# One row of mLSTM forget sums, spread over 128 partitions by TensorE instead of by a DMA from DRAM

## The reference, cut to what matters

```
b = jnp.cumsum(fb, axis=-1)
D = jnp.where(causal, b[..., :, None] - b[..., None, :] + ib[..., None, :], -jnp.inf)
inter = b + m[..., None]
m_t = jnp.maximum(inter, D.max(-1))
s_mat = jnp.exp(D - m_t[..., None]) * jnp.einsum('bhtd,bhsd->bhts', qb, kb)
num = (w_inter[..., None] * jnp.einsum('bhtd,bhde->bhte', qb, C) + jnp.einsum('bhts,bhse->bhte', s_mat, vb))
```

## Time and profile before

| quantity | value |
|---|---|
| median of 3 runs | 1026.46 us (1025.17 to 1029.41) |
| the profiled execution, its own time | 1025.17 us |
| its span, first to last instruction | 1023.4 us |
| TensorE, matmuls | 953.4 us busy, 93% |
| VectorE | 602.2 us busy, 59% |
| ScalarE | 457.2 us busy, 46% of the span |
| mean granted TensorE clock | 0.981 |

### The profile page before, as it was taken

How to read it: one execution, slowest core, us unless ns; L and a number is a source line. 1 busy time by engine, 2 the same in 40 slices (tenths; PEclk the granted TensorE clock), 3 DMA queues, 4 the chain that set the end, 5 groups by cost and what they waited for, 6 DMA issues and landing times.

```text
span 1023.4 us, 14224 instructions
## 1 busy us (share of the span) xinstructions
PE 953.4 (93%) x4965; PEld 754.4 (74%) x4965; DVE 602.2 (59%) x1100; ACT 457.2 (45%) x811; POOL 173.0 (17%) x145
## 2 busy tenths in 40 slices
PE   2399999899999899998999998999999999988995
PEld 1367877677877688776788776788778888866883
DVE  2854786564875566865657856553653333264766
ACT  1133456554475463665554765434743222251221
POOL 1101021322032231122420132311100000001220
PEclk9689999999999999999999999999999999999998
DMA  8702121011311102211113111115712111233232
GB/s 287 250 11 67 43 63 42 22 34 29 93 40 41 31 20 61 72 40 31 30 31 93 42 31 33 31 50 165 242 58 73 50 42 41 93 105 101 83 105 100
DMA packets 78083, 73.64 MB, mean 72 GB/s; under 512 B 4792, under 2 KB 66360, under 8 KB 78044
## 3 DMA queue, kind: packets, MB, share of 16 engines
q1 hardware_dynamic: 73116, 58.31, 19.8%
q0 software_dynamic: 2624, 8.54, 2.5%
q10 hardware_dynamic: 2304, 6.29, 1.6%
HBM read 64.59 MB, written 8.40 MB: 71 GB/s over the span
## 4 chain that ended last, share of the span: by engine, by line
PE 86%; DVE 4%; ACT 4%; issue 3%; DMA 2%; SPq 1%; POOL 0%; ACTq 0%; DVEq 0%; POOLq 0%
PE bank L617 45%; PE bank L597 9%; PE bank L599 9%; PE bank L598 9%; PE bank L732 3%; PE bank L716 3%; PE bank L701 2%; PE bank L686 1%; DMA x_rows<-in_x 1%; ACT rem L982 1%; DMA a_raw<-in_w_ada 1%; PE bank L703 1%; PE bank L702 1%; DVE a_acc L1302 1%; PE bank L759 1%
## 5 line engine op out<-in xcount | busy, mean ns | idle before, releaser
L617 PE MATMUL bank<-hH,wH 128*128 128x512 f32 x704 | 288.7, 410 | 0.6 <-DVE wL L1316 0.6
L617 PE MATMUL bank<-hH,wL 128*128 128x512 f32 x704 | 276.7, 393 | 0.0
L617 PE MATMUL bank<-hL,wH 128*128 128x512 f32 x704 | 275.5, 391 | 0.0
L556 POOL TENSOR_TENSOR ez<-ez,rem 128x512 f32<-128x512 f32 (+3 forms) x96 | 135.0, 1425 | 423.4 <-DVE rem L1478 423.4
L1316 DVE SCALAR_TENSOR_TENSOR wL<-w_raw,wH 128x512 fp32r<-128x512 f32 (+1 forms) x122 | 94.0, 772 | 142.3 <-ACT wH L901 141.2
L617 PEld LDWEIGHTS bank<-hH,wH 128*128 128x128 f32 x704 | 132.5, 188 | 35.7 <-issue 10.6
L617 PEld LDWEIGHTS bank<-hH,wL 128*128 128x128 f32 x704 | 132.2, 188 | 29.3
L617 PEld LDWEIGHTS bank<-hL,wH 128*128 128x128 f32 x704 | 132.7, 189 | 24.6 <-issue 1.0
L901 ACT ACTIVATE wH<-w_raw 128x512 fp32r<-128x512 f32 (+1 forms) x122 | 75.5, 621 | 103.1 <-PE bank L599 76.2
L1478 DVE TENSOR_TENSOR_SCAN rem<-rem,ones 128x512 f32<-128x512 f32 (+3 forms) x96 | 88.5, 964 | 28.5 <-ACT rem L986 28.5
L994 ACT ACTIVATE at<-bank 128x512 f32<-128x512 f32 (+3 forms) x96 | 46.2, 481 | 42.3 <-PE bank L716 42.3
(11 more groups left out here) (234 smaller groups left out, 1466.1 us busy)
## 6 DMA issues: line engine op xcount, KB each, us to landing
w_raw<-in_w_in SPq DMA_DIRECT2D x104, 256.0 KB, 2.9
a_raw<-in_w_ada SPq DMA_DIRECT2D x16, 512.0 KB, 4.6
x_rows<-in_x SPq DMA_DIRECT2D x8, 512.0 KB, 7.7
raw<-in_w_ada POOLq DMA_DIRECT2D x8, 512.0 KB, 5.9
x_in<-in_x SPq DMA_DIRECT2D x8, 512.0 KB, 4.0
out_y<-res SPq DMA_DIRECT2D x8, 512.0 KB, 2.9
raw<-in_w_out SPq DMA_DIRECT2D x10, 256.0 KB, 4.3
m_w<-bm_scratch ACTq DMA_DIRECT2D x4, 512.0 KB, 4.0
```

Of the source, the lines that this page charges most:

```text
L556: g.tensor_tensor(e, e, r, ALU.mult).then_inc(a_done[h], 1)
L617: ins = t.matmul(proj_ps[half][:], w, a, start=(r == 0), stop=(r == JOB_MM // 2 - 1))
```

## The change

The store to DRAM and the four DMAs that read it 128 times go away, with their semaphores. In their place DVE copies, among the per-head columns, the selector of head i (`sel_cur`, 128 x 128, ones in row i and row 32 + i). After the first 48 projection matmuls of an iteration, and ahead of `scores(i, 0)`, TensorE multiplies rows 0 to 31 of `sel_cur` with rows 0 to 31 of `bm`, in two plain float32 matmuls of 512 columns, one into each misc bank. This puts row i of bm on all 128 partitions. There are 21 fills an iteration now.

DVE reads the banks in `chunk_weights`, which moves from slot 0 to a place ahead of slot 0 and of `cap_odds(i, 0)`: one addition of 512 columns from each bank, each followed by a wait for itself, then the minimum over 1024. The wait for `yml_stored` moves to DVE with it. ACT's exponential moves from slot 1 to slot 0, and DVE's masking from slot 1 to slot 0, ahead of `pair_gate`.

```diff
-        M_PRO, M_PER = [10, 9], [20, 20]
-        F_V, F_MK, F_MV, F_CHUNK, F_HN = 0, 1, 2, 3, 19
+        M_PRO, M_PER = [10, 9], [21, 21]
+        F_V, F_R, F_MK, F_MV, F_CHUNK, F_HN = 0, 1, 2, 3, 4, 20
...
-            pool.wait_ge(bm_made, 1)
-            pool.dma_start(bm_dram[:, :], bm[0:NH, :]).then_inc(bm_out, 16)
...
                 project(i, 24, PRE)
+                pe.wait_ge(h_cols, i + 1)
+                for n in range(2):
+                    pe.wait_ge(m_drained[n], m_count(n, i, F_R))
+                    t.matmul(misc_ps[n][:], sel_cur[0:32, :], bm[0:32, halves(n)], start=True, stop=True)\
+                        .then_inc(m_filled[n], 1)
                 for s in range(NS):
...
-            def load_forget_row(i):
-
-                row = bm_dram[i:i + 1, :] if isinstance(i, int) else bm_dram[bass.ds(i, 1), :]
-                act.wait_ge(bm_out, 16)
-                act.wait_ge(yml_stored, i * 16 + 16)
-                act.dma_start(m_w[:].rearrange("p c t -> p (c t)"), row.broadcast_to((P, S))).then_inc(bm_in, 16)
-
             def place1(i, s):
                 if s == 0:
-                    load_forget_row(i)
-                if s == 1:
                     act.wait_ge(w_sum, i + 1)
                     a.activation(m_w[:], m_w[:], ACT.Exp).then_inc(w_exp, 1)
...
-                link.wait()
+                link(v.tensor_copy(sel_cur[:], sel_all[:, bass.ds(i, 1), :].rearrange("p a b -> p (a b)")))
...
             def chunk_weights(i):
 
-                dve.wait_ge(bm_in, i * 16 + 16)
-                u = h_tok[:, 0, :].unsqueeze(2).to_broadcast((P, NC, P))
-                link(v.tensor_tensor(m_w[:], m_w[:], u, ALU.add))
+                dve.wait_ge(yml_stored, i * 16 + credit)
+                for n in range(2):
+                    dve.wait_ge(m_filled[n], m_count(n, i, F_R) + 1)
+                    u = h_tok[:, 0, 4 * n:4 * n + 4].unsqueeze(2).to_broadcast((P, 4, P))
+                    v.tensor_tensor(m_w[:, 4 * n:4 * n + 4], misc_ps[n][:].rearrange("p (a b) -> p a b", a=4), u,
+                                    ALU.add).then_inc(m_drained[n], 1)
+                    dve.wait_ge(m_drained[n], m_count(n, i, F_R) + 1)
                 v.tensor_scalar(m_w[:], m_w[:], 0.0, None, ALU.min).then_inc(w_sum, 1)
...
                 if s == 0:
+                    mask_chunk_weights(i)
                     pair_gate(i)
-                    chunk_weights(i)
                 if s == 1:
-                    mask_chunk_weights(i)
                     conv_sum(i, 2)
...
                 tasks(i, 24, PRE, last)
+                chunk_weights(i)
                 for s in range(NS):
```

More of the change, by code:

```diff
@@ L191, in build_kernel @@
     ysb_dram = nc.dram_tensor("ysb_scratch", (NH, P, S), F32, kind="Internal").ap()
-    bm_dram = nc.dram_tensor("bm_scratch", (NH, S), F32, kind="Internal").ap()
     yml_dram = nc.dram_tensor("yml_scratch", (NH, P, S), F32, kind="Internal").ap()
@@ L265, in build_kernel @@
         h_col = it("h_col", [P, 56])
+        sel_cur = it("sel_cur", [P, P])
         stat = it("stat", [P, NC, 6])
@@ L325, in build_kernel @@
         m_drained = [sem(f"misc_drained{n}") for n in range(2)]
-        bm_made, bm_out, bm_in = sem("bm_made"), sem("bm_out"), sem("bm_in")
         dec_filled, dec_drained = sem("dec_filled"), sem("dec_drained")
@@ L1411, in _ @@
             dve.sem_inc(yml_stored, credit)
-            dve.sem_inc(bm_made, 1)
             link.base, link.k = link.base + link.k, 0
```

## The result

The changed kernel takes 1037.79 us at the median of four runs (1036.62 to 1040.06), against 1025.82 for the kernel before on the same chip (1024.82 to 1029.41). The ratio is 1.011, with a 95% interval of 1.0092 to 1.0129: slower by 12.0 us, where 7.3 had been forecast and 1037.0 was the end of the range. The kernel before spreads over 6 us, and its four runs here lie low: in the larger groups of the experiments its median is 1027.4, 1028.8 and 1028.2. Against those the changed kernel's 1037.8 would be 9 to 10.4 us more, so part of the 12 may be the luck of these four. The profiled execution of the changed kernel took 1035.96 us, 10.8 more than the one of before.

The account below looks back on a forecast made before the run. TensorE was taken to bound the kernel: 6.9 us of passes plus 0.4 for shape gave 7.3, so 1032.5 on the profiled execution or 1033.8 on the median. The forecast was 1033.2 us, range 1029 to 1037.

Parts of the forecast that it names:

- What bounds the kernel: From the projections ahead of slot 0 to the first turned weights, TensorE alone sets the end; added matmuls are paid.
- What goes away, at 0: Removing the store, four DMAs and their issue gains 0, since the DMA was hidden behind VectorE's work of slot 0.
- The passes at 0.43: Ahead of slot 0, two selector matmuls are four passes of 0.43 us, 1.72 an iteration, 6.9 us in all.
- The reason given for 32 rows: In the selector matmuls, contracting fewer rows does not shorten the number of columns that stream through.
- rival 2: Selector passes over 32 rows are cheap, 0.23 us or less: 1029 to 1030.5, or 1027 to 1028.5; chance 0.10.
- The change of shape: One more entry into another array shape ahead of slot 0: 0.1 us a visit, 0.4 in all, at most 1.2.
- VectorE's side, covered: VectorE's extra 0.5 us an iteration is covered; the cap of slot 0 comes 0.8 late, within 6.5 us of slack.
- Rival 3: VectorE's block ahead of slot 0 becomes a wait: 1036, up to 1038 us; chance 0.12.
- the one on TensorE's stops: Stops for turned weights, 13.9 us in 12 waits in later slots, shift with TensorE because their chain starts with its matmuls.
- The list of what would prove me wrong: Passes at 0.23 or less, pitch growth under 1.5 or over 2.2 us, or a new TensorE wait in slots 0 to 3.
- rival 1: TensorE's stops, 3.5 us an iteration, swallow the added 1.8: 1025 to 1027 us, not slower; chance 0.09.

Follow-up runs that it names:

- Experiments 1: Kernel before, keeping its DMA and order, plus two unread plain float32 32-row matmuls of 512 columns an iteration: 1038.84 us, ratio 1.0108.
- experiment 2: Kernel before with DMA issued at iteration start and the addition, exponential and masking moved as in the change, no matmul added: 1027.13 us, ratio 0.9998.
- experiment 6: Changed kernel with the selector matmuls over all 128 rows, the selector holding 0.5: 1036.38 us, ratio 1.0091 to the kernel before.
- experiments 5: Kernel before plus ten unread fp32r matmuls of 512 columns in the stop of slot 7: 1024.58 us, ratio 0.9959.
- 10: Kernel before, unchanged, profiled once more: 1026.57 us.
- 11: Kernel before, unchanged, profiled yet once more: 1028.28 us.
- 4: Kernel before plus eight unread fp32r matmuls of 512 columns over 128 rows an iteration, ahead of slot 0: 1038.35 us, ratio 1.01.
- 9: Kernel before plus four unread fp32r matmuls over 128 rows an iteration, ahead of slot 0: 1031.68 us, ratio 1.0028.
- 3: Changed kernel plus ten unread fp32r matmuls of 512 columns in the stop of slot 7: 1030.47 us, ratio 1.003 to the kernel before.
- 7: Kernel before with nine more projection matmuls in slot 7, taken from the end of the iteration: 1017.64 us, ratio 0.9903.
- 8: Changed kernel with nine more projection matmuls in slot 7, taken from the end of the iteration: 1026.42 us, ratio 0.9983 to the kernel before.

## Why the prediction was wrong, point by point

**What bounds the kernel: right.** The four visits are paid in full. No TensorE wait came up in slots 0 to 3.

**What goes away, at 0: right.** Experiments 1 and 2 have the same times as the change and the kernel before, each with the DMA. The DMA was hidden, and it costs nothing to keep.

**The passes at 0.43: right.** 6.9 us of the sum, and a visit over 128 rows measures 1.72. The reason given for 32 rows holds too (experiment 6), so rival 2 is out. The change of shape was mis-sized: 0.1 a visit by the earlier trace rows, 0.19 measured. It makes the visits 7.6 instead of 7.3. The prediction took one gap of 0.1 for the shape of 32 rows, and there are two: in the changed kernel the first selector pass starts 0.32 us after the last projection matmul instead of 0.23, and the second 0.53 after the first instead of 0.43.

**VectorE's side, covered: right, and cheaper than I said.** The timeline of the kernel before at the cap of slot 0, and that of the changed kernel, beside the earlier trace rows:

```profile
127.24 0.48 DVE L1465 SCALAR_TENSOR_TENSOR ez<-ez,earlier 128x128 f32<-128x128 f32 x2
```

```profile
125.25 1.50 DVE L1541 TENSOR_TENSOR m_w<-bank,h_tok 128x512 f32<-128x512 f32 x2
126.78 0.70 DVE L1544 TENSOR_SCALAR m_w<-m_w 128x1024 f32<-128x1024 f32 x1
127.39 0.49 DVE L1456 SCALAR_TENSOR_TENSOR ez<-ez,earlier 128x128 f32<-128x128 f32 x2
...
134.57 0.23 DVE L1453 TENSOR_SCALAR ez<-ez 128x128 f32<-128x128 f32 x1
```

The scores of slot 0 start at 125.2, so the cap of slot 0 is 2.2 us behind them, against 127.24 - 125.28 = 2.0 before: late by 0.2 where I had 0.8. (By its own rows the prediction should have had 0.5: 129.5, less the 127.24 + 1.8 at which the cap would have stood.) The cap of slot 1 is 9.4 behind them, against 9.9. Rival 3 named 1036 to 1038, and the time fell there, but by another mechanism; experiment 2 has its moved steps at 0.9998.

**The step that failed** is the one on TensorE's stops: "If TensorE comes later to that point, so does the whole chain." That is true of the chain, and the stops did stay at 13.8 us. I concluded that they leave the sum alone, and so the sum has nothing for them, without a reason that covers the clock. What a stop does to TensorE's clock does not move along with the chain. The missing term is 3 x 1.58 = 4.7 us in the profile. The list of what would prove me wrong named a pitch that grows by "more than 2.2"; it grew by 3.0.

The stop that matters was also misread. The earlier trace rows calls the one that ends at 177.79 + 0.26 the largest, by the length of the chain outside TensorE; but TensorE had projection matmuls to do there, and idled for 0.4 us. The stop of 2.9 is in slot 7, and its chain is this one:

```profile
194.71 0.24 PE bank L752 x2
...
195.24 1.23 DVE sig L1501
...
199.62 0.28 ACT at L994
...
199.94 0.44 PE bank L716 x2
```

It begins with TensorE's own matmuls too, so what the prediction concluded about the length of the stops, and against rival 1, stands.

**What I should have read.** The profile of before has no fall in the loop. But it has two in the stages behind it, each after a stop about as long as the one in the loop: 2.37 us up to 914.47, and 2.98 up to 941.71. About 1 us after the first, the matmuls start 0.43 us apart, and the granted clock of the window is 0.50:

```profile
914.47 0.47 PE L597 MATMUL bank<-hH,yH 128*128 128x512 f32 x1 [2.37 <-DVE yL L1786]
914.78 0.40 PE L598 MATMUL bank<-hL,yH 128*128 128x512 f32 x1
...
915.88 0.63 PE L599 MATMUL bank<-hH,yL 128*128 128x512 f32 x1
916.31 0.63 PE L597 MATMUL bank<-hH,yH 128*128 128x512 f32 x1
```

```profile
915.50:918.90 3.40, 3.40 (x10) 0.50 0.46 148
```

So the trace of before already had stops of 2.4 and 3.0 us with the low clock behind them, and four of 2.9 in the loop that were spared. And the runs beside it spread from 1025.17 to 1029.41, and the profile was taken on the fastest. In this kernel most of the spread is the clock's (experiments 5, 10 and 11), so one profile without a fall said little of the median. The stop of 2.9 us stood in the earlier trace rows, and I used it as a place where time might be won, never as one where it might be lost. The Trainium skill (TensorE: Matmul & The Clock Gate, HAM oscillation — how this bites in real kernels) describes a kernel whose TensorE falls to the low clock after each wait for a transfer, and pays for it in every tile. The traces agree that the fall stands at a stop: 0.3 us behind its end in the changed kernel's iteration 1, and before its end in the two double falls. Here the wait is for ScalarE, not for a transfer, and the same stop is at times followed by a fall and at times not.

**What stays open.** Stops of the same 2.94 us are followed by a fall in three of four iterations of one profile and in none of another. In the nine profiles whose stop is not filled, 2 of 16 slots 7 have a fall where no time was added (before, experiments 2, 10 and 11), and 16 of 20 where it was (the change, 1, 4, 6 and 9); with the stop filled (3, 5, 7 and 8) it is none of 16. So that added time brings falls, and that filling the stop ends them, is shown. The rule by which a given stop is hit or spared is not worked out here, so the number of falls could not have been forecast, only bounded: none to one an iteration, 0 to 6.3 us, and 1.1 more for each that lasts twice as long. With that bound the forecast would have been 1033 to 1040 or a little more.

## What to carry to other kernels

On a kernel bound by TensorE, a broadcast on TensorE is no saving if the DMA that it replaces was hidden: it is charged at 0.43 us for each 512 columns and pass, over 32 rows as over 128. Read TensorE's stops twice: once for their own length, and once for the clock behind them; a long one in a loop is a term of its own in every sum that changes the loop's timing. And the best answer to such a stop, of those tried here, is to move work into it that the engine has to do anyway: nine matmuls moved in a hand-written order gave 1.0%, nearly as much as the broadcast lost.

## What the runs showed of the hardware that was not expected

- At a stop of TensorE of 2.94 us, and behind the loop of 2.37 us, the granted clock went from 2.4 to 1.2 GHz for 3.4 us in some executions and not in others. In slot 7 that costs 1.4 to 1.6 us; in two profiles it was low for 6.8 us at one stop, for 2.7.
- Forty useless matmuls made the changed kernel more than 7 us faster, and the kernel before 4 us faster.
- A plain float32 matmul of 512 columns is two passes of 0.43 us over 32 rows as over 128 rows; going from 128 rows to 32 and on to 64 costs 0.19 us more than going from 128 to 64.
